# Expert weights in a mixture-of-experts kernel on one Trainium2 core: three transfers per expert instead of six

## The reference, cut to what matters

```python
logits = xt @ router_w + router_b
top_val, top_idx = lax.top_k(logits, 4)
comb = jax.nn.softmax(top_val, axis=-1)
...
def expert_block(args):                       # the tokens of one expert
    tok_b, e = args
    xb = xpad[tok_b]
    hu = xb @ w1[e] + b1[e]                   # 1024 -> 2048
    x_glu = jnp.minimum(hu[:, 0::2], 7.0)
    x_lin = jnp.clip(hu[:, 1::2], -7.0, 7.0)
    act = x_glu * jax.nn.sigmoid(1.702 * x_glu) * (x_lin + 1.0)
    return act @ w2[e] + b2[e]                # 1024 -> 1024
```

## Time and profile before

| | before |
|---|---|
| median of 3 runs | 1353.26 us (1351.74, 1353.26 and 1355.78) |
| span of the profiled execution | 1350.4 us |
| that execution's own time | not given apart; the three runs lie 1.3 to 5.4 us above the span |
| TensorE busy | 1284.6 us, 95% of the span |
| VectorE busy | 391.3 us, 29% |
| ScalarE busy | 188.3 us, 14% |
| moved by DMA | 471.71 MB, mean 349 GB/s |

### The profile page before, as it was taken

How to read it: one execution, slowest core, us unless ns; L and a number is a source line. 1 busy time by engine, 2 the same in 40 slices (tenths; PEclk the granted TensorE clock), 3 DMA queues, 4 the chain that set the end, 5 groups by cost and what they waited for, 6 DMA issues and landing times.

```text
span 1350.4 us, 17457 instructions
## 1 busy us (share of the span) xinstructions
PE 1284.6 (95%) x6549; PEld 625.8 (46%) x6550; DVE 391.3 (29%) x982; ACT 188.3 (14%) x401; POOL 48.3 (4%) x48
## 2 busy tenths in 40 slices
PE   7999999999999999999999999999999999999997
PEld 5788878898753333323333322333333323333332
DVE  1599565632152211112111111211121111121112
ACT  1110123522030110001100000100010000011001
POOL 1020012220000000000000000000000000000000
PEclk9999999999999999999999999999999999999999
DMA  9998650008349999999999999599999999999995
GB/s 332 345 375 300 222 187 1 1 6 338 125 152 382 429 428 428 428 430 428 430 427 429 427 430 429 248 431 429 427 427 428 431 429 428 428 427 429 430 428 244
DMA packets 61015, 471.71 MB, mean 349 GB/s; under 512 B 4093, under 2 KB 4410, under 8 KB 36154
## 3 DMA queue, kind: packets, MB, share of 16 engines
q1 hardware_dynamic: 60160, 469.62, 84.1%
q10 hardware_dynamic: 538, 1.13, 0.3%
q0 software_dynamic: 288, 0.55, 0.2%
HBM read 470.23 MB, written 1.05 MB: 349 GB/s over the span
## 4 chain that ended last, share of the span: by engine, by line
PE 54%; DMA 41%; DVE 1%; SPq 1%; ACT 1%; issue 1%; DVEq 0%
DMA ring<-in_exp_w_dram 40%; PE bank L1339 18%; PE bank L806 12%; PE bank L1374 6%; PE bank L1235 2%; DMA ring<-in_ada_w_dram 2%; PE bank L1024 2%; PE bank L1386 2%; PE bank L1309 2%; PE bank L900 1%; PE bank L1333 1%; PE bank L1157 1%; PE bank L1141 1%; PE bank L1154 1%; SPq L487 1%
## 5 line engine op out<-in xcount | busy, mean ns | idle before, releaser
L1339 PE MATMUL bank<-ring,work 128*64 128x512 f32 x2112 | 470.5, 596 | 43.4 <-DMA ring<-in_exp_w_dram 43.4
L1339 PEld LDWEIGHTS bank<-ring,work 128*64 128x64 f32 x2112 | 144.5, 137 | 364.9 <-issue 278.3
L1374 PE MATMUL bank<-ring,work 128*64 128x512 f32 x1056 | 234.1, 595 | 0.9 <-ACT work L749 0.5
L1374 PEld LDWEIGHTS bank<-ring,work 128*64 128x64 f32 x1056 | 73.0, 137 | 137.8 <-issue 136.5
L756 ACT ACTIVATE work<-work 128x256 f32<-128x256 f32 x66 | 27.5, 416 | 761.0 <-DVE work L1865 761.0
L1865 DVE TENSOR_SCALAR work<-bank 128x256 f32<-128x256 f32 x66 | 27.7, 419 | 346.3 <-PE bank L1339 346.3
L806 PE MATMUL bank<-region_h,ring 128*128 128x256 f32 x576 | 126.6, 380 | 0.0
L806 PEld LDWEIGHTS bank<-region_h,ring 128*128 128x128 f32 x576 | 108.8, 190 | 14.4
L1895 DVE TENSOR_TENSOR work<-bank,work 128x512 f32<-128x512 f32 x33 | 22.8, 692 | 313.8 <-PE bank L1374 313.8
L1386 PE MATMUL bank<-work 64*128 64x512 f32 x264 | 65.6, 615 | 0.8 <-DVE work L1895 0.8
L1309 PE MATMUL bank<-qkv,work 128*64 128x512 f32 x264 | 62.3, 592 | 0.2 <-DVE work L1803 0.2
(11 more groups left out here) (304 smaller groups left out, 956.0 us busy)
## 6 DMA issues: line engine op xcount, KB each, us to landing
ring<-in_exp_w_dram SPq DMA_DIRECT2D x190, 2048.0 KB, 23.3
ring<-in_ada_w_dram SPq DMA_DIRECT2D x12, 2048.0 KB, 12.5
ring<-in_w_in_dram SPq DMA_DIRECT2D x11, 2048.0 KB, 12.7
ring<-in_w_in_dram SPq DMA_DIRECT2D x4, 1024.0 KB, 16.7
ring<-in_w_gdn_out_dram SPq DMA_DIRECT2D x2, 2048.0 KB, 11.6
ring<-in_w_out_dram SPq DMA_DIRECT2D x2, 2048.0 KB, 16.5
ring<-in_exp_w_dram SPq DMA_DIRECT2D x4, 1024.0 KB, 23.7
ring<-in_w_pool_out_dram SPq DMA_DIRECT2D x1, 2048.0 KB, 8.0
```

The source lines that it names most:

```text
L1339: mm = nc.tensor.matmul(bank[b][h * SLOTS:(h + 1) * SLOTS, :], xT[:, c % 4, c // 4, :], quads(slot_as(q, 2)[:, i, b * D:(b + 1) * D], h), ...
L1374: mm = nc.tensor.matmul(bank[2][o * SLOTS:(o + 1) * SLOTS, :], actT[:, b, c, h, :], slot_as(4 + b, 2)[:, h, lo:lo + 512], start=(b + h + c ...
```

## The change

For experts 1 to 30, SP loads two neighbouring slots in one transfer: three transfers of 4 MB in place of six of 2 MB, with one piece of 32 KB in each partition. Slots 0 and 1 take the first four rows of w1 of each partition, slots 2 and 3 the other four, slots 4 and 5 the whole of w2. A transfer waits for both slots to be free and raises `landed` of the even slot only, so TensorE waits on that one for both chunks; the semaphores of the odd slots are counted in the first and last expert alone, which are still loaded singly (`stream_singly`; now slots 3 and 5 of both in two halves).

So that w2 can be one piece of 32 KB per partition, partition p has to hold the eight rows 8p to 8p + 7 of w2. The hidden features are dealt out to match: half b is no longer a half of w1's columns but, in every sixteen columns, eight; `quads` takes four columns of every sixteen. The b1 rows are therefore loaded in full into both places (32 rows of 8 KB twice, before 32 rows of 4 KB twice).

```diff
--- before.py
+++ after.py
@@ -232,7 +232,7 @@
         y_nat = take(512)
         gt2_row = take(512)
         b2_rows = take(512)
-        b1_rows = take(1024)
+        b1_rows = take(2048)
         fin_g = take(D)
         fin = q_of.rearrange("p h s -> p (h s)").rearrange("p (t d) -> p t d", t=T)
         fin_sq = xn2
@@ -271,8 +271,7 @@
         early_in = sem("early_in")
         b_in = sem("b_in")
         fin_in = sem("fin_in")
-        hidden_in = sem("hidden_in")
-        last_in = sem("last_in")
+        first_half_in = {s: sem(f"first_half_in{s}") for s in (3, 5)}
         out_done = sem("out_done")
         landed = [sem(f"landed{i}") for i in range(RING)]
         upper_in = [sem(f"upper_in{i}") for i in range(2)]
@@ -415,6 +414,9 @@
         def cut(w, lo, n=CW):
             return w[0, :, lo:lo + n].rearrange("(c p) n -> p c n", p=P)
 
+        def slot_pair(i):
+            return ring[:, i:i + 2, :, :].rearrange("p i c n -> p (i c n)")
+
         def slot_as(i, c):
             return ring[:, i, :, :].rearrange("p c n -> p (c n)").rearrange("p (c n) -> p c n", c=c)
 
@@ -439,8 +441,10 @@
         USES = len(chunks) // RING
         assert len(chunks) % RING == 0
 
+        w1_pairs = exp_w1.rearrange("l e (p b c) n -> (l e) p b (c n)", p=P, b=2)
         w1_dram = exp_w1.rearrange("l e (p c) n -> (l e) p c n", p=P)
-        w2_dram = exp_w2.rearrange("l e (b p h c) n -> (l e) b p h (c n)", b=2, h=2, p=P)
+        w2_dram = exp_w2.rearrange("l e (p b h c) n -> (l e) b p h (c n)", b=2, h=2, p=P)
+        w2_both = exp_w2.rearrange("l e (p r) n -> (l e) p (r n)", p=P)
 
         def w_slot(n, j, k):
 
@@ -493,27 +497,36 @@
                 if n == RING - 1:
                     sp.dma_start(consts[:, 2 * P + 1:CONST_W], const[:, 2 * P + 1:CONST_W]).then_inc(tables_in, 16)
 
-            def stream(e, blocks_before):
+            def stream_singly(e, blocks_before):
+
                 for s in range(RING):
                     src = w1_dram[e, :, 2 * s:2 * s + 2, :] if s < 4 else w2_dram[e, s - 4]
                     sp.wait_ge(used[s], blocks_before + USES)
-                    if isinstance(e, int) and e == E - 1 and s in (3, 5):
-                        sp.dma_start(slot_as(s, 2)[:, 0, :], src[:, 0, :]).then_inc(landed[s], 16)
-                        sp.dma_start(slot_as(s, 2)[:, 1, :], src[:, 1, :]).then_inc(hidden_in if s == 3 else last_in, 16)
+                    if s in (3, 5):
+                        sp.dma_start(slot_as(s, 2)[:, 0, :], src[:, 0, :]).then_inc(first_half_in[s], 16)
+                        sp.dma_start(slot_as(s, 2)[:, 1, :], src[:, 1, :]).then_inc(landed[s], 16)
                     else:
                         sp.dma_start(slot_as(s, 2), src).then_inc(landed[s], 16)
 
-            stream(0, 0)
+            def stream_in_pairs(e, blocks_before):
+
+                for s in (0, 2, 4):
+                    sp.wait_ge(used[s], blocks_before + USES)
+                    sp.wait_ge(used[s + 1], blocks_before + USES)
+                    src = w1_pairs[e, :, s // 2, :] if s < 4 else w2_both[e]
+                    sp.dma_start(slot_pair(s), src).then_inc(landed[s], 16)
+
+            stream_singly(0, 0)
             sp.wait_ge(vec_x1, 4)
             for i in range(2):
                 at = slice(i * SLOTS, i * SLOTS + E)
-                sp.dma_start(b1_rows[at, :], exp_b1[0][:, i * D:(i + 1) * D]).then_inc(b_in, 16)
+                sp.dma_start(b1_rows[at, :], exp_b1[0]).then_inc(b_in, 16)
                 sp.dma_start(b2_rows[at, :], exp_b2[0][:, i * 512:(i + 1) * 512]).then_inc(b_in, 16)
             sp.dma_start(fin_g, final_norm_g.partition_broadcast(P)).then_inc(fin_in, 16)
             sp.wait_ge(vec_route, 1)
             with sp.Fori(1, E - 1) as e:
-                stream(e, first_block_of(sp, e))
-            stream(E - 1, first_block_of(sp, E - 1))
+                stream_in_pairs(e, first_block_of(sp, e))
+            stream_singly(E - 1, first_block_of(sp, E - 1))
             for i in range(2 * T):
                 cut_ = slice((i % 2) * 512, (i % 2 + 1) * 512)
                 sp.wait_ge(vec_out, i + 1)
@@ -1322,8 +1335,8 @@
                     mm = nc.tensor.transpose(bank[b][:, c * P:(c + 1) * P], act_nat[:, b, c * P:(c + 1) * P], ident)
                 mm.then_inc(pe_actT, 1)
 
-            def quads(columns, h):
-                return columns.rearrange("p (f h c) -> p h f c", h=2, c=4)[:, h]
+            def quads(columns, b, h):
+                return columns.rearrange("p (f b h c) -> p b h f c", b=2, h=2, c=4)[:, b, h]
 
             def bias(n):
                 pe.wait_ge(act_xT, n + 1)
@@ -1331,18 +1344,37 @@
                 for h in range(2):
                     for b in range(2):
                         nc.tensor.matmul(bank[b][h * SLOTS:(h + 1) * SLOTS, :], onehot[b * SLOTS:b * SLOTS + E, :],
-                                         quads(b1_rows[b * SLOTS:b * SLOTS + E, :], h), start=True, stop=False)
+                                         quads(b1_rows[b * SLOTS:b * SLOTS + E, :], b, h), start=True, stop=False)
 
             def hidden(n, q, i, b):
                 c = 2 * q + i
                 for h in range(2):
                     mm = nc.tensor.matmul(bank[b][h * SLOTS:(h + 1) * SLOTS, :], xT[:, c % 4, c // 4, :],
-                                          quads(slot_as(q, 2)[:, i, b * D:(b + 1) * D], h),
+                                          quads(slot_as(q, 2)[:, i, :], b, h),
                                           start=False, stop=(c == KC - 1))
                 return mm
 
+            def chunk_arrived(s, e):
+
+                if s % 2 == 0:
+                    pe.wait_ge(landed[s], 16 * (e + USES + 1))
+                elif isinstance(e, int):
+                    pe.wait_ge(landed[s], 16 * (e // (E - 1) + USES + 1))
+                else:
+                    pe.wait_ge(landed[s], 16 * ((e + 1) // E + USES + 1))
+
+            def half_arrived(s, e):
+
+                if isinstance(e, int):
+                    pe.wait_ge(first_half_in[s], 16 * (e // (E - 1) + 1))
+                else:
+                    pe.wait_ge(first_half_in[s], 16 * ((e + 1) // E + 1))
+
             def w1_chunk(n, q, e=0, last=False):
-                pe.wait_ge(landed[q], 16 * (e + USES + 1))
+                if q == 3:
+                    half_arrived(q, e)
+                if not last:
+                    chunk_arrived(q, e)
                 if q < 3:
                     for i in range(2):
                         for b in range(2):
@@ -1351,7 +1383,7 @@
                 elif last:
                     for b in range(2):
                         hidden(n, q, 0, b)
-                    pe.wait_ge(hidden_in, 16)
+                    chunk_arrived(q, e)
                     hidden(n, q, 1, 0).then_inc(pe_hu, 1)
                     hidden(n, q, 1, 1).then_inc(used[q], 1)
                 else:
@@ -1364,10 +1396,13 @@
 
             def w2_chunk(n, b, e, last=False):
                 pe.wait_ge(act_actT, 2 * n + b + 1)
-                pe.wait_ge(landed[4 + b], 16 * (e + USES + 1))
+                if b:
+                    half_arrived(5, e)
+                if not (last and b):
+                    chunk_arrived(4 + b, e)
                 for h in range(2):
                     if last and b and h:
-                        pe.wait_ge(last_in, 16)
+                        chunk_arrived(5, e)
                     for c in range(2):
                         for o in range(2):
                             lo = c * D + o * 512
```

## The result

The changed kernel takes 1359.09 us (median of 4 runs, 1357.61 to 1359.83) against 1352.74 us before (median of 4): a ratio of 1.0047 with a 95% interval of 1.0032 to 1.0062. The forecast was 1359.0 us, against 1353.26 of the three runs then known. The profiled execution took 1359.33 us, with a span of 1356.9 us in place of 1350.4. The agreement to 0.1 us is partly luck: between the medians lie 6.35 us where 5.7 were forecast, while the kernel before came out 0.5 us lower than it was known.

A forecast was written before the change was run, and what follows sets the result against it. The prediction took the loads to set the pace, at 29.37 us per expert against TensorE's 26.8. Costs of 12.1 us less 6.4 us of gain gave +5.7 us, a median of 1359.0 us; range 1352 to 1367.

The forecast's parts named there:

- The gain: Expert loads: 32 KB pieces in place of 16 KB take an expert from 29.37 to 29.15 us, -6.4 us in all.
- The line through the two rates of the earlier trace: Straight line through DMA rates of 2 KB (388 GB/s) and 16 KB pieces (428): 9 ns fixed per piece, 0.03683 ns per byte.
- the rival that they are cut back: Expert loads: transfers cut back to 16 KB pieces, or edges not costing 9 ns; no gain, +12.1 us, 1365.4 us; chance 0.13.
- The start: Loop start: SP's first issue waits for the second chunk too, at 409.0 in place of 407.34 us; +1.7 us.
- The hole: Two-block expert: the stretch from w1 landing to SP's next issue grows from 20.1 to 27 us; +7.0 us.
- The end: Behind the last landing on the chain: two w1 chunks are left for TensorE in place of one; +3.4 us.
- The queue does not run dry: Steady experts: pairs come free at least 10 us before DMA wants them; one TensorE wait of 2.2 us per expert.
- Dealing of the features and bias load: TensorE's reads of 16 bytes in every 64 and 256 KB more b1 rows: taken as 0 us.
- the estimate from the ceiling: Expert loads at the 435.2 GB/s limit: at most 0.46 us saved per expert, 14 us in all, sum -1.7 us.
- The rival of the lower clock: TensorE: a 2.2 us wait might bring 1.2 GHz, losing 1.7 us at hole and end, up to 1362.4 us; chance 0.04.
- The sign: Within the experts: the prediction is wrong if TensorE's granted clock leaves 1.00 (2.4 GHz).
- the three costs: Later loop start (1.7 us), longer hole at the two-block expert (7.0), later TensorE behind the last landing (3.4): 12.1 us.

The follow-up runs named there:

- the six small matmuls: The changed kernel plus six small matmuls into a free bank before each loop block's third w1 chunk: 1361.03 us, ratio 1.0072 to the kernel before.

## Why the prediction was right

By its own steps:

1. *The gain.* 29.15 us per expert were put down, 29.14 measured, and 6.6 us in all against 6.4. The line through the two rates of the earlier trace rows held for a size twice the larger one. The same view for the changed kernel, 600 to 700 us, reads 432 GB/s (431 forecast):

```profile
DMA packets 1479, 43.22 MB, mean 432 GB/s; under 512 B 160, under 2 KB 160, under 8 KB 160
```

   Packets in this stretch fell from 2935 to 1479: the pieces really are 32 KB, and the rival that they are cut back is out. The ceiling of 435.2 GB/s that the Trainium skill gives (DMA: Bandwidth & Descriptors, Where 436 GB/s comes from) was not passed by the level of any slice in the expert stage: the highest is 433. (The 437 of the 3.6 us stretch above goes with a DMA share of 1.01, so it is not exact enough to be held against it.) As the prediction worked out from this ceiling, there was little left to win: of the 0.46 us per expert of its estimate 0.23 came. The "no more than 1 MiB per transfer" that it cites from the Trainium skill (same page, Rules for kernel authors) is the least size that the rule asks for, not a limit, and the runs agree: beyond it, 4 MB transfers were no faster than 2 MB ones at the same 16 KB pieces, 29.37 us both.
2. *The start*: +1.7 put down, +1.8 measured. The issue itself came at 410.04 and not at 409.0, since bias 0 began 0.9 us later in this profile.
3. *The hole*: +7.0 put down, +6.9 measured. The chain in it has exactly the pieces named.
4. *The end*: +3.4 put down, +3.5 measured. The run with 29 and 30 single shows it by itself.
5. *The queue does not run dry*: right. The one wait per expert was 2.12 us (after a stretch at the lower clock 0.4), against 2.2 put down. The run with w1 whole shows the same account tipping over where the margin is used up.
6. *Dealing of the features and bias load*: nothing, as put down, and shown by the run that has them alone.

So the mechanism held, and each size to 0.2 us. That the median agrees to 0.1 us is luck: the span was 6.5 us longer, not 5.7, mostly because of the later bias 0, and the changed kernel's median lay 2.2 us above its span, where 2.9 had been carried over. Two slips in the prediction's text changed nothing: the steady level begins at the fourteenth slice, the thirteenth has 382 GB/s, and with the 29.67 experts of its own sum the estimate from the ceiling is -1.5 us, not -1.7.

The rival of the lower clock was half right. I had given as a sign of a wrong prediction that the clock leaves 1.00 within the experts. It did, nine times in this profile, and the sum held all the same, because the steady stretch hides 1.7 us and none of the nine fell on the hole or the end. The runs with expert 1 and with 14 to 16 single show the price where one does, 1.7 us each, as it was worked out. The sign was badly chosen; the price was right. That the waits are a consequence of the coarser grain is clear from the run with the new dealing and single loads, which has waits in two parts and a mean granted clock of 0.995 over the span, like the kernel before (0.996; the change 0.984).

My expectations of the experiments failed at one step above all (the price of the six small matmuls and the time of an expert with w1 whole were too low besides). I took each cost to be local to its expert. But TensorE's lateness from a pair is carried into the next expert and made good at only about 2.5 us per expert, so a single expert 30 or 15 gets less than was put down, or nothing. In the run of 4 MB transfers with 16 KB pieces the three costs as measured (12.2 us) and the 1.5 us of lower clock at the end make 13.7, against 13.3 found; nothing larger than 0.4 us is left unexplained there. What stays open is why a wait of 2.1 us is followed by the lower clock in nine cases of fifteen and not in the other six, and so how often the changed kernel meets it at the hole or the end: each profile is one execution.

## What to carry to other kernels

When loads set the pace, a faster rate is paid per byte, but a coarser grain is paid only where the pipeline starts, stalls or ends: count the places on the path and price each with the chain of waits. Here 0.22 us times 30 lost to 1.8 + 6.9 + 3.5 us; coarse transfers in the steady stretch with fine ones at the breaks, and for the expert ahead of each break, won, by 0.3% on this input. Before a transfer is made larger still, compare the time its slots take to come free with the time of what is queued behind it: from 10 us to spare to the queue running dry was one step here.

## What the runs showed of the hardware that was not expected

- In the changed kernel the granted clock fell to 0.50 after nine of the fifteen waits of 2.1 us before a third w1 chunk, and after none of the ten shorter ones (0.4 to 1.0 us). In the kernel before, the two waits of 0.9 and 1.3 us per expert, with 3.65 us of work between them, were never followed by it.
- After such a drop TensorE is 1.7 us late, so the next wait is short (0.43 us before the chunks at 841.38, in place of 2.1), and in no profile of these kernels with 4 MB pairs did a drop follow at once. So the drops keep themselves in bounds here, and cost 1.7 us only where one meets a break.
- By an estimate, the fixed part of a piece, 9 ns by the straight line from 2 and 16 KB, held at 32 KB (0.23 us less per expert is 9.6 ns for each of the 24 pieces saved). The number of transfers, six or three per expert, could not be seen in the rate.
